# Moving weight loads, PSUM banks and a history cast in a two-layer convolutional trunk on eight cores

## The reference, cut to what matters

```
h = rmsnorm(x);  p = h @ w_in           # 7 column groups of 1024
u  = a_val * sigmoid(a_gate)            # group A
ca = causal_dwconv(u, history, width 31) + bias
ya = silu(layernorm_per_head(ca)) * silu(z_a)
v  = C * hb                             # group B
yb = Bg * causal_dwconv(v, history, width 3) * silu(z_b)
x  = x + concat(ya, yb) @ w_out
```

## Time and profile before

| | |
|---|---|
| runs shown | 1317.79, 1312.59, 1313.7 us, median 1313.7 |
| the profiled execution | 1315.9 us, span 1314.3 us on core 1, the slowest |
| spans of cores 0 to 7 | 1302.0, 1314.3, 1307.9, 1302.0, 1298.2, 1302.9, 1302.1, 1314.3 |
| PE busy | 1196.8 us, 91% |
| DVE, ACT, POOL busy | 778.8 (59%), 507.9 (39%), 239.8 (18%) |
| mean of one L501, L750, L727, L398 on DVE | 655, 581, 595, 592 ns |
| weight loads, median issue to landing | 5.6 us (w_in), 5.0 us (w_out) |

### The profile page before, as it was taken

One profiled execution on the slowest core, in us unless ns is written; L12 is line 12 of the kernel. 1 busy time (PEld: TensorE's weight loads), 2 busy tenths in 40 slices (PEclk: granted clock), 3 DMA queues, 4 the chain that ended last, 5 costly groups with the idle time before them and its releaser, 6 DMA issues.

```text
span 1314.3 us, 23097 instructions; the slowest of 8 cores (1298.2 to 1314.3 us)
## 1 busy us (share of the span) xinstructions
PE 1196.8 (91%) x7706; PEld 631.9 (48%) x7706; DVE 778.8 (59%) x1470; ACT 507.9 (39%) x812; POOL 239.8 (18%) x341
## 2 busy tenths in 40 slices
PE   4798989999899999999989999998889999999984
PEld 1354444544455555554435545454445554555441
DVE  2555466544576576666864455655457656666686
ACT  4576643666221101112446665356622110111242
POOL 0044323343010000000003333334300000000000
PEclk9999999999899999999989999999989999999997
DMA  9756742565234214221326864256422321312127
GB/s 239 153 103 112 121 80 56 102 117 99 29 76 81 33 13 104 33 33 33 41 41 113 131 112 83 56 101 116 91 29 33 64 33 17 49 33 33 17 107 167
DMA packets 98756, 101.27 MB, mean 77 GB/s; under 512 B 34448, under 2 KB 79760, under 8 KB 98576
## 3 DMA queue, kind: packets, MB, share of 16 engines
q1 hardware_dynamic: 76800, 57.56, 21.1%
q0 software_dynamic: 20880, 37.89, 18.9%
q10 hardware_dynamic: 960, 4.34, 1.0%
HBM read 92.93 MB, written 13.37 MB: 81 GB/s over the span
## 4 chain that ended last, share of the span: by engine, by line
PE 70%; ACT 8%; DMA 8%; DVE 5%; issue 4%; SPq 3%; DVEq 0%; ACTq 0%
PE ps L332 64%; DMA rep<-ubuf 7%; PE ps L447 3%; ACT sq L351 2%; SPq L584 2%; PE ps L466 1%; DMA x_sb<-xT 1%; ACT L494 1%; SPq L284 1%; DVE acc L702 1%; DVE x_sb L384 1%; ACT rstd_t L494 1%; PE ps L340 1%; DVE tt_t L501 1%; DVE ubuf L610 1%
## 5 line engine op out<-in xcount | busy, mean ns | idle before, releaser
L332 PE MATMUL ps<-h_sb,wsl 128*128 128x424 bf16 (+1 forms) x4400 | 827.0, 344 | 19.0 <-ACT sz_t L724 17.5
L332 PEld LDWEIGHTS ps<-h_sb,wsl 128*128 128x128 bf16 x4400 | 427.0, 98 | 386.1 <-issue 46.1
L332 PE MATMUL ps<-y_sb,wsl 128*128 128x424 bf16 (+1 forms) x1280 | 240.4, 346 | 12.5 <-ACT sz_t L624 4.6
L398 DVE TENSOR_TENSOR x_sb<-x_sb,ps 128x424 f32<-128x424 f32 (+1 forms) x320 | 181.0, 592 | 43.7 <-PE ps L332 25.8
L314 POOL DMA_DIRECT2D wsl<-w_in_r x112 | 60.1, 540 | 720.0 <-PE ps L332 493.2
L332 PEld LDWEIGHTS ps<-y_sb,wsl 128*128 128x128 bf16 x1280 | 126.0, 99 | 123.2 <-issue 25.2
L739 ACT ACTIVATE th_t<-ps 128x424 f32<-128x424 f32 (+1 forms) x80 | 41.8, 523 | 252.5 <-PE ps L332 218.8
L724 ACT ACTIVATE sz_t<-ps 128x424 f32<-128x424 f32 (+1 forms) x80 | 41.8, 523 | 227.8 <-PE ps L332 204.2
L702 DVE SCALAR_TENSOR_TENSOR acc<-ubuf,cw_b_sb,acc 128x424 f32<-128x424 bf16 (+2 forms) x176 | 106.6, 606 | 18.4
L610 DVE SCALAR_TENSOR_TENSOR ubuf<-th_t,ps 128x424 bf16<-128x424 f32 (+1 forms) x80 | 46.2, 578 | 119.0 <-PE ps L332 71.3
L750 DVE TENSOR_TENSOR ubuf<-ps,th_t 128x424 bf16<-128x424 f32 (+1 forms) x80 | 46.5, 581 | 93.6 <-PE ps L332 93.3
(11 more groups left out here) (50 smaller groups left out, 713.7 us busy)
## 6 DMA issues: line engine op xcount, KB each, us to landing
wsl<-w_in_r POOLq DMA_DIRECT2D x112, 256.0 KB, 5.6
rep<-ubuf SPq DMA_DIRECT2D x256, 109.0 KB, 3.9
wsl<-w_out_r POOLq DMA_DIRECT2D x32, 256.0 KB, 5.0
x_sb<-xT SPq DMA_DIRECT2D x16, 424.0 KB, 13.6
y_fm<-x_sb SPq DMA_DIRECT2D x16, 424.0 KB, 3.0
rep<-ubuf SPq DMA_DIRECT2D x128, 47.0 KB, 2.6
hista<-hist_a SPq DMA_DIRECT2D x16, 255.5 KB, 3.5
oa_copy<-sa_orig ACTq DMA_DIRECT2D x2, 1664.0 KB, 10.2
```

The lines of the kernel that those rows point to most:

```text
L332: ins = e.matmul(bank(bk, n), lhsT=l_, rhs=r_, start=(i == 0), stop=(i == len(pairs) - 1))
L398: P.op("dve", (lambda e, bk=bk, m=m: e.tensor_tensor(out=x_sb[:, m, c0:c0 + n], in0=x_sb[:, m, c0:c0 + n], in1=bank(bk, n), op=ALU.add)), ...
```

## The change

Five edits are made.
1. In an A step, the load at b = 3 goes, and so does the one ahead of the sums at b = 4. In their place two loads stand between the two half sums, after all three slots of the stage are given up. Stage 0 of layer 0 gets these two as well.
2. In the combined stage all four projections of a step have banks of their own, and `b0_rot` is fitted to them.
3. The silu of zb is issued by a hook inside `pipe(1, b)`, ahead of the single's product and silu at b = 0.
4. The variances of the pair at b = 1 go to banks 1 and 7 in A steps, and stay in 6 and 7 in the combined stage.
5. In the first stage, four rmsnorm products and the cast of the history into `usam` (L416) go behind the casts of the first convolution.

```diff
-                    st_var_mm(s, (6 if b == 1 else 2) + i)
+                    st_var_mm(s, ((1, 7) if b == 1 and alone else (6, 7) if b == 1 else (2, 3))[i])
...
             if b % 2 == 0:
                 while q_y:
                     st_y(q_y.pop(0))
+            if hook is not None:
+                hook()
             if b == 0 and single:
                 st_tt(single[0])
                 st_silu(single[0])
...
         if b == NB - 1:
-            w_free(2)
-            w_load(0 if g == NB - 1 and not st["l"] else 1, gate=[th_r[st["th"]]])
+            w_free(3)
             a_samp(st["j"], 0)
+            w_load(2)
             a_samp(st["j"], 1)
             if st["j"] + 1 < 8:
                 a_hist_load(st["l"], st["j"] + 1)
-            w_free(1)
         else:
             if b == 2:
                 w_load((0, 2, 3, 3, 2, 3, 3, 3)[st["j"]], gate=[u_r[2]])
-            elif b == 3:
-                w_load(1, gate=[th_r[st["th"]]])
...
-            bzb, bgb, bgc, bhb = (0, 1, 0, 1) if g % 2 else (2, 3, 2, 3)
-            pipe(0, b)
+            bzb, bgb, bgc, bhb = ((2, 3, 0, 1), (0, 1, 2, 3), (0, 1, 2, 3), (2, 3, 0, 1), (0, 1, 2, 3))[b]
+            pipe(0, b, False)
...
+        def silu_z():
+            P.op("act", (lambda e: e.activation(out=sz_t[:, isz, 0:n], in_=bank(bzb, n), func=AF.Silu)),
+                 reads=[bank_r[bzb]], writes=[sz_r[isz]])
         if g is not None:
-            pipe(1, b)
+            pipe(1, b, False, silu_z)
+        else:
+            silu_z()
...
         evac(3)
-        rms_apply(0, 4, rs_of[4], range(4, 8))
         w_load(1, gate=[u_r[3]])
-        a_hist(0, 0)
         def pipe4(at, b):
             if at == 0:
                 first.append(q_conv.pop(0))
                 st_conv(first[0], (6, 7))
+                rms_apply(0, 4, rs_of[4], range(4, 8))
+                a_hist(0, 0)
...
-    b0_rot = ((0, 1, 6, 7, 2, 3), (2, 3, 4, 5, 6, 7, 0, 1), (0, 1, 4, 5, 2, 3), (2, 3, 4, 5, 0, 1), (0, 1, 4, 5, 6, 7, 2, 3))
+    b0_rot = ((2, 3, 6, 7, 0, 1), (0, 1, 4, 5, 6, 7, 2, 3), (0, 1, 4, 5, 2, 3), (2, 3, 4, 5, 0, 1), (0, 1, 4, 5, 6, 7, 2, 3))
```

More of the change, by code:

```diff
@@ L484, in st_rstd @@
         if pair:
-            vb, n = pair[0]["vb"], BLOCKS[pair[0]["b"]][1]
+            n = BLOCKS[pair[0]["b"]][1]
             for t, s in enumerate(pair):
                 s["rstd"], s["rstd_r"] = rstd_t[:, t, 0:n], rstd_r[t]
-                ops.append((rstd_t[:, t, 0:n], bank(vb + t, n), [bank_r[vb + t]], [rstd_r[t]]))
+                ops.append((rstd_t[:, t, 0:n], bank(s["vb"], n), [bank_r[s["vb"]]], [rstd_r[t]]))
         for s in single:
@@ L519, in build_nc, with pipe @@
     cur = {}
-    def pipe(at, b):
+    def pipe(at, b, alone=True, hook=None):
         single = [cur["s"]] if "s" in cur else []
@@ L720, in b_step @@
             b_hist(l, j)
+        isz = b if b < NB - 1 else NB - 1 + j % 2
+        def silu_z():
+            P.op("act", (lambda e: e.activation(out=sz_t[:, isz, 0:n], in_=bank(bzb, n), func=AF.Silu)),
+                 reads=[bank_r[bzb]], writes=[sz_r[isz]])
         if g is not None:
-            pipe(1, b)
-        isz = b if b < NB - 1 else NB - 1 + j % 2
-        P.op("act", (lambda e: e.activation(out=sz_t[:, isz, 0:n], in_=bank(bzb, n), func=AF.Silu)),
-             reads=[bank_r[bzb]], writes=[sz_r[isz]])
+            pipe(1, b, False, silu_z)
+        else:
+            silu_z()
         proj(s_gb, b, bgb)
```

## The result

The changed kernel takes 1280.7 us (median of 4, 1278.9 to 1282.0) against 1313.9 (1312.6 to 1317.8): ratio 0.9741, 95% interval 0.9718 to 0.9765. Forecast were 1275 us and a range of 1263 to 1290. A repeat of the same kernel (e13_after_again) gave 0.9738 (0.9714 to 0.9761).

The account below looks back on a forecast made before the run. PE sets the end, so removed waits count in full. Gains of 15.2 (copies), 1.6 (clock), 4 (chain), 5.2 (first stage) and 14.0 us (combined stages) sum to 40: from 1315.9 to 1275.9, median 1273.7, set at 1275; range 1263 to 1290.

Parts of the forecast that it names:

- I put the cost at nothing: A stages: the two loads between the half sums are done before block 1's copies are issued, costing 0 us.
- all ten waits go: A stages: convolutions no longer wait for shifted copies, a gain of 15.2 us, lower bound 9.
- the 1.6 us for the clock: Convolution that had waited 2.97 us for copies: without the wait PE's clock stays up, gaining 1.6 us.
- some 9 us: A stages: distance between the issue of the two loads and that of block 1's copies, given against a delay.
- Rival C: Convolution at b = 3: loads delay its copies, 41 us at 4.6 us delay; chance 0.03 slower, 0.03 about unchanged.
- The 4 us of gain: A stages, b = 1: shorter waits on the chain before the pair's second variance; bounds 9 gained, 6 lost.
- The gap between the sums: A stages: POOL issues DMAs for 1.1 us between sums, freeing the y products; chain about 2 us shorter.
- Rival A: A stages: the chain before the variance takes the copies' place, 4 us gain becomes 6 loss, 1285 us; chance 0.17.
- step 2: Combined stage: DVE's eight adds of 0.70 us end late, the mean waits 2.3 us; -0.8 us per layer.
- Step 0: Combined stage: the silu and copy waits go, but the output weight lands late; 0.7 us gained per layer.
- Step 1: Combined stage: gc and hb run during ACT's work, `out_block` starts 5.6 us earlier after a remaining 1.1 us wait.
- Steps 3 and 4: Combined stage: the 1.53 us wait on the silu of zb goes in the first; the second had no wait.

Follow-up runs that it names:

- e13_after_again: The changed kernel unaltered, run again as a control: 1281.4 us, ratio 0.9738 to the kernel before.
- e6: Changed kernel with both moved weight loads behind the second half sum instead of between the sums: 1319.9 us, ratio 1.0023 to the kernel before.
- e7: Changed kernel with the two weight loads ahead of both half sums instead of between them: 1274.5 us, ratio 0.9662 to the kernel before.
- e1: Changed kernel with the weight loads back at b = 3 and ahead of the sums, the other edits kept: 1297.9 us, ratio 0.9836.
- e10: e1 with the sample sums on POOL cut to two taps in place of 31: 1281.3 us, ratio 0.9715.
- e5: Changed kernel with the pair's variances at b = 1 back in banks 6 and 7 in all steps: 1280.2 us, ratio 0.9716.
- e7_loads_ahead: Full name of e7, its first series: changed kernel with the two loads ahead of both half sums, 1274.5 us, ratio 0.9662.
- e14_ahead_again: The kernel of e7 run a second time, beside a repeat of the changed kernel: 1276.3 us, ratio 0.9699 to the kernel before.

## Why the prediction was right, and where it was not
**Direction, size and likeliest case** were right: 33 us measured in the medians, 37.0 in the profiled executions, 40 in the sum. But two errors of the sum cancelled, one of 8 us too much in the A stages and one of 6 too little in the combined stages. That the total came so close is luck.

**Edit 1, the copies: the step that failed.** "I put the cost at nothing" was wrong, and so was "all ten waits go". On core 1 they fell at b = 0 from 15.7 to 5.0 us, but 7.2 us came at b = 3, in stages that had had slack there: 3.6 us net for a term of 15.2; the 1.6 us for the clock came (the convolution at 125.61 took 1.62 us). In the mean of the cores the copy waits went from 12.1 to 6.1 us. Nor can the waits be added up for the time: on core 0 they went from 9.4 to 1.2 us, yet its two stretches with the A stages became only 5.9 us shorter, and its waits on the silu of z rose from 4.6 to 7.0. The landing of block 1's copies in stage 1, before and after (issued from 80.0 and from 75.8 us), shows it:
```profile
DMA to landing us min/median/max: 3.2/3.6/3.9
```
```profile
DMA to landing us min/median/max: 5.0/5.2/6.4
```
With 6.4 in place of 3.9 the slack of 1.7 is gone. The copies of block 0 just ahead of them (issued from 74.5 and from 69.9 us) were hit harder:
```profile
DMA to landing us min/median/max: 3.2/3.7/3.8
```
```profile
DMA to landing us min/median/max: 7.2/7.7/8.3
```
And the two loads themselves, issued at 68.6 and 69.1 us, took longer than the 5.6 us that I had read from the table:
```profile
DMA to landing us min/median/max: 7.2/7.8/8.4
```
So they were in flight until about 77 us. Three things were left out of my working. First, other transfers are issued in the same stretch: the load of the history (L413, 255.5 KB against 256.0 for a weight load), directly beside the two loads, and the copies of block 0, which land late and still lie ahead of block 1's. Second, "some 9 us" between the loads and block 1's copies was a distance in the old timeline, which held the waits that the change removes. In stage 2 the loads were issued at 99.6 and 100.1 us and the copies from 105.5 on: 6 us. Third, the loads there landed 7.1 and 8.5 us after their issue, so behind the first of these copies; "done before the copies of block 1 are issued" was false. Which of the three weighs most was not tried. Rival C was the right mechanism at about a fifth of its size (7.2 us against 41). e6 shows that a kernel with the loads 6 us later is no faster than before; I had given C 3 in 100, and as much to a time unchanged by it.

**The waits behind it: right size, wrong reason.** The 4 us of gain came out as 7.0 on core 1 (variance waits 9.3 to 2.3) and 2.4 over the cores. The gap between the sums was named as the cause; e7 without a gap has nearly the same waits (4.0 us). The pair's y products are early because the convolution and its casts are, and so miss the second sum: on core 1 they took 2.1 to 3.8 us in seven stages before, and at most 1.4 after, but for the first stage. The single's product meets it now (1.51 us at 101.52 us), and that costs the variance little. e1 gives most of it back (5.2 us), and e10 shows that the sum is what they collide with. The lock for a whole instruction that the Trainium skill states (SBUF — State Buffer, who interferes with whom) fits e10's 1.10 against 3.71 us. That the gap shortens the chain was my own reading. Rival A is refuted.

**Edit 4** is worth nothing that can be measured, as forecast (e5).

**Edit 5:** 4.7 us for 5.2 at its place. The mean started at 58.15 (58.45 forecast), but part of the lower clock stayed: 2.27 us for 8 matmuls, between 1.6 and 2.98, at a mean granted clock of 0.68.

**Edits 2 and 3:** 10.1 us in each layer for 7.0. The mis-sized term is step 2 (-0.8 forecast, +0.9 measured: output blocks 1 and 2 are 13.68 us apart, 14.56 before). I had taken 0.70 us for each add of `out_block` from the earlier trace rows. There DVE kept pace with PE; it was not DVE's own rate. When the adds start late, they run without waiting:
```profile
326.15 0.59 DVE L753 TENSOR_TENSOR ubuf<-ps,th_t 128x424 bf16<-128x424 f32 x1
326.65 4.48 DVE L398 TENSOR_TENSOR x_sb<-x_sb,ps 128x424 f32<-128x424 f32 x8
```
Eight in 4.48 us are 0.56 each, so DVE caught up, and the mean waited 0.90 us as before, not 2.3. Step 0: the output weight landed 3.8 us after its issue, not 4.8, and the wait was 1.26 us (and 1.64), where 2.2 were forecast. Step 1: a wait of 1.11 us at full clock, as forecast, and 5.9 us gained for 5.6. Steps 3 and 4 gave 1.8 and 0.4 us for 1.5 and 0.

**The slowest core.** From core 1 a span of 1274.3 had followed, and 1277.3 was measured. Core 4 came to 1268.6, below its 1272.9, for it kept 1.5 of its 6.1 us of copy waits but shared the larger gain of the combined stages. The medians gained 4 us less than the profiled execution did.

A version that beats both kernels is e7: the two loads ahead of the sums, 1274.5 and 1276.3 us in two series of executions.

## What to carry to other kernels
A transfer that is taken out of one crowded stretch is put into another: count there everything that is issued, whichever queue issues it, and measure distances in the timeline as it will be, without the waits that the change removes. A row in which an engine keeps pace with a slower one gives the slower one's rate; for how fast it can catch up, take the mean of one instruction. When one wait goes, look at what the late operation had been pushed into; in e1 two products that met a sum on another engine made 4.7 us of waits, beside 16.6 on the late copies themselves.

## What the runs showed of the hardware
- Two f32 products of DVE on SBUF took 1.10 us with POOL idle and 3.71 us beside a sum of POOL.
- After 2.38 us without work PE's clock fell for a while in e7 (granted clock 0.50 from 127.0 to 130.1 us on core 1; the convolution took 3.02 us, 1.62 at full clock). After 2.95 us in combined step 0 of layer 1 before, the granted clock was 1.00 and 16 matmuls ran in 3.03 us, the 2.4 GHz level. So the length of the gap alone does not tell here.
- In one execution of the same program copy waits were 1.2 us on core 0 and 12.1 on core 1, and they are not fixed to a core: in e7_loads_ahead core 4 had none and core 1 6.6 us, in the same kernel as e14_ahead_again core 4 had 6.3 and core 1 2.3. Why, was not looked for.
